# S5 set-up of a hybrid decoder trunk: rotation frames, cosine, a sum of C and the mean on other engines and in another order

## What is computed

```python
def s5_mixer(u, a_re, a_im, log_dt, b_re, b_im, c_re, c_im, d_skip, w_glu, b_glu):
    lam = lax.complex(jnp.minimum(a_re, LAMBDA_RE_MAX), a_im)      # 64 groups x 64 states
    dt = jnp.exp(log_dt)[:, None]
    lam_bar = jnp.exp(lam * dt)
    b_bar = ((lam_bar - 1.0) / lam)[:, :, None] * b_c
    bu = ...                                  # ug (16 channels of a group) x b_bar, complex
    _, states = lax.associative_scan(combine, (a, bu), axis=1)    # s_t = lam_bar * s_(t-1) + bu_t
    y = real(states) @ c_re - imag(states) @ c_im + d_skip * u
    y = gelu(y)
    z = y @ w_glu + b_glu
    val, gate = split(z, 2)
    return val * sigmoid(gate)

def reference(...):
    h = x
    h = h + s5_mixer(rmsnorm(h, g), ...) ; h = h + sq_relu_mlp(rmsnorm(h, g), ...)
    h = h + swa_sink_attention(...)      ; h = h + sq_relu_mlp(rmsnorm(h, g), ...)
    return rmsnorm(h, norm_final)
```

## Time and profile before

| | |
|---|---|
| median of 3 runs | 1054.39 us (1054.22 to 1054.98) |
| the profiled execution | 1052.76 us, of which the span of its instructions is 1050.9 us |
| busy share of the span | PE 98%, PEld 80%, POOL 66%, DVE 53%, ACT 22% |
| mean granted TensorE clock | 0.992 |
| chain that ended last, by engine | PE 86%, DVE 4%, ACT 4%, issue 2% |

### The profile page before, as it was taken

One profiled execution on the slowest core, in us unless ns is written; L12 is line 12 of the kernel. 1 busy time (PEld: TensorE's weight loads), 2 busy tenths in 40 slices (PEclk: granted clock), 3 DMA queues, 4 the chain that ended last, 5 costly groups with the idle time before them and its releaser, 6 DMA issues.

```text
span 1050.9 us, 15733 instructions
## 1 busy us (share of the span) xinstructions
PE 1026.3 (98%) x5738; PEld 839.0 (80%) x5738; DVE 560.9 (53%) x645; ACT 229.8 (22%) x512; POOL 694.8 (66%) x568
## 2 busy tenths in 40 slices
PE   9889999999999999999999999999999999999996
PEld 4677888888888888888887777888888888888886
DVE  7993446677317515613855775568761472273125
ACT  7863111110001000101312777221100010010011
POOL 8996866687667766766646330778776676677650
PEclk9899999999999999999999999999999999999998
DMA  6123332232222323222222110233223322223212
GB/s 248 39 44 124 114 102 93 77 120 100 93 89 99 100 100 100 89 94 99 100 80 100 41 51 12 80 106 101 99 96 100 100 100 100 83 97 100 100 61 80
DMA packets 35904, 97.51 MB, mean 93 GB/s; under 512 B 11144, under 2 KB 13704, under 8 KB 35600
## 3 DMA queue, kind: packets, MB, share of 16 engines
q1 hardware_dynamic: 35856, 96.83, 27.9%
HBM read 92.36 MB, written 2.10 MB: 90 GB/s over the span
## 4 chain that ended last, share of the span: by engine, by line
PE 86%; DVE 4%; ACT 4%; issue 2%; SPq 1%; DMA 1%; DVEq 0%; POOL 0%; POOLq 0%
PE ps L1265 23%; PE ps L1267 23%; PE ps L1266 23%; PE ps L1211 2%; PE ps L1213 2%; PE ps L1212 2%; SPq L314 1%; ACT s_sb L647 1%; PE ps L1422 1%; PE ps L1408 1%; PE ps L1396 1%; DMA toep<-k_even 1%; DVE negm L1028 1%; PE ps L1328 1%; PE ps L1327 1%
## 5 line engine op out<-in xcount | busy, mean ns | idle before, releaser
L438 POOL TENSOR_TENSOR w_lo<-raw,w_hi 128x1024 fp32r<-128x1024 f32 x164 | 414.8, 2529 | 13.7
L1265 PE MATMUL ps<-hid,w_hi 128*128 128x512 f32 x704 | 275.9, 392 | 0.0
L1267 PE MATMUL ps<-hid,w_lo 128*128 128x512 f32 x704 | 274.1, 389 | 0.0
L1266 PE MATMUL ps<-hid,w_hi 128*128 128x512 f32 x704 | 274.0, 389 | 0.0
L350 POOL TENSOR_TENSOR gate_sb<-gate_sb 128x1 f32<-128x1 f32 x164 | 41.0, 250 | 308.2 <-PE ps L1267 269.4
L1265 PE MATMUL ps<-act,w_hi 128*128 128x512 f32 x464 | 180.6, 389 | 0.0
L1267 PE MATMUL ps<-act,w_lo 128*128 128x512 f32 x464 | 180.5, 389 | 0.0
L1266 PE MATMUL ps<-act,w_hi 128*128 128x512 f32 x464 | 180.5, 389 | 0.0
L435 POOL TENSOR_SCALAR w_hi<-raw 128x1024 fp32r<-128x1024 f32 x164 | 173.3, 1057 | 0.0
L1267 PEld LDWEIGHTS ps<-hid,w_lo 128*128 128x128 f32 x704 | 132.1, 188 | 27.8
L1265 PEld LDWEIGHTS ps<-hid,w_hi 128*128 128x128 f32 x704 | 132.2, 188 | 27.6 <-issue 0.5
(11 more groups left out here) (218 smaller groups left out, 1062.4 us busy)
## 6 DMA issues: line engine op xcount, KB each, us to landing
raw<-panels_in SPq DMA_DIRECT2D x164, 512.0 KB, 3.2
xy<-xu_in SPq DMA_DIRECT2D x4, 512.0 KB, 7.5
out<-h SPq DMA_DIRECT2D x8, 256.0 KB, 2.2
prm<-prm_in SPq DMA_DIRECT2D x1, 1280.0 KB, 5.8
h<-x_rows_in SPq DMA_DIRECT2D x1, 1280.0 KB, 12.9
h<-x_rows_in SPq DMA_DIRECT2D x1, 768.0 KB, 7.2
dd<-dd_in SPq DMA_DIRECT2D x1, 256.0 KB, 5.8
toep<-k_even SPq DMA_DIRECT2D x4, 64.0 KB, 2.4
```

The lines of the kernel that those rows point to most:

```text
L438: nc.gpsimd.tensor_tensor(w_lo[:, s, :], raw[:, s % 2, :], w_hi[:, s, :].bitcast(F32), ALU.subtract).then_inc(w_split, 1)
L1265: mm(ps[:, bank, :], w_hi[:, s, w], x[:, 0, k, :], start=(k == 0), stop=False)
L1266: mm(ps[:, bank, :], w_hi[:, s, w], x[:, 1, k, :], start=False, stop=False)
L1267: last = mm(ps[:, bank, :], w_lo[:, s, w], x[:, 0, k, :], start=False, stop=(k == KT - 1))
```

## The change

It touches the set-up and the first two octets alone. Every other stage, every DMA and its issue stay.

- Cosine: instead of sin(pi x), its square and 1 - 2 sin^2, ACT takes Abs and then Sin with scale -2 pi and a bias of a quarter turn from a tile (`quarter`). That is one ACT operation less in each frame, one DVE operation less in the set-up (L725), and a small Sin and Square for the one power that still needs sin^2.
- The copy of the turns (`turn8`) goes ahead of the set-up's first Sin.
- Whole turns: for frames 1 to 3 DVE only rounds, and PE adds minus the whole turns in PSUM with a second matmul (`part_turns`, with the tile `minus`); ACT reads PSUM. Frame 0 is rounded and subtracted by DVE in the set-up, ahead of the input factors, and ACT does it between the squares.
- `c_sum` is formed by two matmuls on PE and a copy on ACT, not by POOL.
- The mean is reduced from PSUM bank 0 into PSUM, after `project_mul(1)`.
- `decay` is made in two halves, after the squares and in octet 1.
- The matmuls on idle data are four at the start and no others.
- New order: POOL makes the weights of octet 0 ahead of `project_im(0)`, and `minus`, the product of `dd`, `project_im(1)` and one product of octet 1 stand ahead of the wait for the mean; DVE and PE take octet 2's projection and fold ahead of `run_states(1)` and `outputs(0)`.

```diff
--- before.py
+++ after.py
...
-SETUP_ARG, SETUP_EXP, SETUP_PH, SETUP_INV, SETUP_L, SETUP_X, SETUP_MS = 3, 2, 6, 9, 15, 28, 32
-SETUP_LAG0, SETUP_R8, SETUP_TURN, SETUP_RSTD = 3, 6, 10, 11
+SETUP_ARG, SETUP_EXP, SETUP_PH, SETUP_INV, SETUP_L, SETUP_X, SETUP_MS = 3, 2, 6, 9, 14, 27, 31
+SETUP_LAG0, SETUP_R8, SETUP_TURN, SETUP_SIN, SETUP_COS, SETUP_SQ, SETUP_RSTD = 1, 6, 7, 8, 10, 12, 13
 T_DMA = 16 * J
-WARM = (5, 1, 2)
+WARM = (4, 1)
...
+QUARTER = 1.5707963
...
         sq_sum = ps[:, 4, :]
+        mean_ps = ps[:, 4, 0:2 * NK].rearrange("p (a k) -> p a k", a=2)
         stat = ps[:, 7, :]
-        phases = (t1[:], t2[:, 0], t2[:, 1], acc[:])
+        first_turns = rstd
+        whole = (t1[:], t2[:, 0], t2[:, 1], acc[:])
...
             tt(PR("b_re"), PR("b_re"), PR("g"), mul).then_inc(setup_p, 1)
             pool.wait_ge(setup_p, 2)
             tt(b_sum, PR("b_re"), PR("b_im"), add).then_inc(setup_p, 1)
-            tt(c_sum[:], PR("c_re"), PR("c_im"), add).then_inc(setup_p, 1)
+            wait(pool, s_cst, 16)
+            nc.gpsimd.tensor_scalar(minus[:], ident, -1.0, 0.0, mul, add).then_inc(negated, 1)
             wait(pool, setup_v, SETUP_L)
-            pool.wait_ge(setup_p, 4)
+            weights_mul(0, (1, 2))
+            pool.wait_ge(c_copied, 1)
             weights_mul(0, (0,))
+            weights_sum(0)
             wait(pool, setup_v, SETUP_X)
             project_im(0)
+            wait(pool, s_dd, 16)
+            tt(dd[:, 0], dd[:, 0], dd[:, 1], mul).then_inc(setup_p, 1)
             project_im(1)
-            weights_mul(0, (1, 2))
-            weights_sum(0)
+            weights_mul(1, (0,))
             wait(pool, setup_a, SETUP_RSTD)
             inputs(0)
-            wait(pool, s_dd, 16)
-            tt(dd[:, 0], dd[:, 0], dd[:, 1], mul).then_inc(setup_p, 1)
-            weights_mul(1)
+            weights_mul(1, (1, 2))
             weights_sum(1)
             inputs(1)
-            wait(pool, s_cst, 16)
-            nc.gpsimd.tensor_scalar(minus[:], ident, -1.0, 0.0, mul, add).then_inc(negated, 1)
             project_im(2)
             weights_mul(2)
...
             wait(a, setup_v, SETUP_PH)
-            act_fn(cos_l[:], ph_ps, ACT.Sin, scale=PI_).then_inc(setup_a, 1)
+            act_fn(turn8[:], ph_ps[:, :, J:J + 1].rearrange("p g a -> p (g a)"), ACT.Copy).then_inc(setup_a, 1)
             act_fn(sin_l[:], ph_ps, ACT.Sin, scale=TWO_PI).then_inc(setup_a, 1)
-            a.wait_ge(setup_a, 7)
-            act_fn(sq_ps, cos_l[:], ACT.Square).then_inc(setup_a, 1)
-            act_fn(turn8[:], ph_ps[:, :, J:J + 1].rearrange("p g a -> p (g a)"), ACT.Copy).then_inc(setup_a, 1)
+
+            act_fn(cos_l[:], ph_ps, ACT.Abs).then_inc(setup_a, 1)
+            a.wait_ge(setup_a, SETUP_COS - 1)
+            wait(a, bank_free, 4)
+            act_fn(cos_l[:], cos_l[:], ACT.Sin, scale=-TWO_PI, bias=quarter[:]).then_inc(setup_a, 1)
+            act_fn(sq_ps[:, :, 0:1].rearrange("p g a -> p (g a)"), ph_ps[:, :, 1:2].rearrange("p g a -> p (g a)"), ACT.Sin,
+                   scale=PI_).then_inc(setup_a, 1)
+            a.wait_ge(setup_a, SETUP_SQ - 1)
+            act_fn(sq_ps[:, :, 1:2].rearrange("p g a -> p (g a)"), sq_ps[:, :, 0:1].rearrange("p g a -> p (g a)"), ACT.Square
+                   ).then_inc(setup_a, 1)
...
-            a.wait_ge(setup_a, SETUP_R8)
-            act_fn(decay[:, :, 1:], r8[:].unsqueeze(2).to_broadcast([P, GP, NK - 1]), ACT.Copy).then_inc(decayed, 1)
+            def decays(n):
+                pairs = slice(n * GP // 2, (n + 1) * GP // 2)
+                act_fn(decay[:, pairs, 1:], r8[:, pairs].unsqueeze(2).to_broadcast([P, GP // 2, NK - 1]), ACT.Copy
+                       ).then_inc(decayed, 1)
+
+            def frame(c, parts=range(3)):
+
+                wait(a, frame_left, c + 1)
+                pairs = slice(8 * c, 8 * c + 8)
+                phase = (ps[:, frame_bank(c), :] if c else first_turns).rearrange("p (g k) -> p g k", k=NK)
+                if 0 in parts:
+                    act_fn(sink_[:, pairs], phase, ACT.Sin, scale=TWO_PI).then_inc(frame_a, 1)
+                if 1 in parts:
+                    act_fn(cosk[:, pairs], phase, ACT.Abs).then_inc(frame_a, 1)
+                if 2 not in parts:
+                    return
+                a.wait_ge(frame_a, 3 * c + 2)
+                act_fn(cosk[:, pairs], cosk[:, pairs], ACT.Sin, scale=-TWO_PI, bias=quarter[:]).then_inc(frame_a, 1)
+
             wait(a, turn_mm, 1)
             act_fn(turn_t[:], ps[0:8, 3, :], ACT.Copy).then_inc(turn_copied, 1)
+            wait(a, c_mm, 1)
+            act_fn(c_sum[:], ps[:, 6, :], ACT.Copy).then_inc(c_copied, 1)
             wait(a, s_prm, 16)
+            a.wait_ge(setup_a, SETUP_R8)
...
-                if o % 2 == 1 and o // 2 < SETUP_LAG0:
-                    lag0_weights(o // 2)
-
-            def frame(c):
-
-                wait(a, frame_v, 2 * c + 2)
-                pairs = slice(8 * c, 8 * c + 8)
-                phase = phases[c].rearrange("p (g k) -> p g k", k=NK)
-                act_fn(sink_[:, pairs], phase, ACT.Sin, scale=TWO_PI).then_inc(frame_a, 1)
-                act_fn(cosk[:, pairs], phase, ACT.Sin, scale=PI_).then_inc(frame_a, 1)
-                a.wait_ge(frame_a, 4 * c + 2)
-                act_fn(cosk[:, pairs], cosk[:, pairs], ACT.Square).then_inc(frame_a, 1)
-                a.wait_ge(frame_a, 4 * c + 3)
-                act_fn(cosk[:, pairs], cosk[:, pairs], ACT.Copy, scale=-2.0, bias=1.0).then_inc(frame_a, 1)
-
+                if 3 <= o <= 5:
+                    frame(0, (o - 3,))
+                if o == 6:
+                    lag0_weights(0)
+            decays(0)
...
             act_fn(rstd_u[:, 0], rstd_u[:, 1], ACT.Sqrt).then_inc(setup_a, 1)
             evacuate_v(0)
-            frame(0)
             evacuate_k(0)
             copy_p(1)
             evacuate_v(1)
+            lag0_weights(1)
             frame(1)
             for o in range(NO):
-                if 0 < o < NO - 1:
+                if 1 < o < NO - 1:
                     copy_p(o + 1)
                 if o > 0:
                     gelu(o - 1)
-                if 0 < o < NO - 1:
+                if 1 < o < NO - 1:
                     evacuate_v(o + 1)
                 if o > 1:
                     y_to_lo(o - 2)
                 if o + 1 < NO:
                     evacuate_k(o + 1)
+                if o == 1:
+                    decays(1)
                 if o > 0:
                     y_to_hi(o - 1)
                 if o == 0:
                     frame(2)
+                    copy_p(2)
+                    evacuate_v(2)
+                    lag0_weights(2)
                     frame(3)
                 elif o + 2 < NO:
                     lag0_weights(o + 2)
...
+            nc.vector.memset(quarter[:], QUARTER)
...
-            wait(v, setup_a, 9)
+            wait(v, setup_a, SETUP_SIN)
             link(tt(lim_ps, sin_l[:], mag_ps, mul))
-            link(ts(cos_l[:], sq_ps, -2.0, 1.0, mul, add))
+            wait(v, setup_a, SETUP_COS)
...
+            wait(v, setup_a, SETUP_SQ)
...
+            v.wait_ge(frame_mm, 1)
+            ts(whole[0], ps[:, frame_bank(0), :], ROUND, ROUND, add, sub).then_inc(frame_v, 1)
+            v.wait_ge(frame_v, 1)
+            tt(first_turns[:], ps[:, frame_bank(0), :], whole[0], sub).then_inc(frame_left, 1)
...
             def mean_square():
                 wait(v, sq_used, NO)
-                link(nc.vector.tensor_reduce(rstd_u[:, 0], ps[:, 6, :].rearrange("p (g k) -> p k g", k=NK), AX.X, add))
-                link(ts(rstd_u[:, 0], rstd_u[:, 0], 1.0 / D, EPS, mul, add))
-                link(nc.vector.reciprocal(rstd_u[:, 1], rstd_u[:, 0]))
+                v.wait_ge(p_done, 2)
+                link(nc.vector.tensor_reduce(mean_ps[:, 0], ps[:, 0, :].rearrange("p (g k) -> p k g", k=NK), AX.X, add))
+                link(ts(mean_ps[:, 1], mean_ps[:, 0], 1.0 / D, EPS, mul, add))
+                link(nc.vector.reciprocal(rstd_u[:, 1], mean_ps[:, 1]))
                 assert count[0] == SETUP_MS
 
             def frame(c):
 
-                turned = ps[:, frame_bank(c), :]
                 v.wait_ge(frame_mm, c + 1)
-                wait(v, frame_v, 2 * c)
-                ts(rstd[:], turned, ROUND, ROUND, add, sub).then_inc(frame_v, 1)
-                v.wait_ge(frame_v, 2 * c + 1)
-                tt(phases[c], turned, rstd[:], sub).then_inc(frame_v, 1)
+                ts(whole[c], ps[:, frame_bank(c), :], ROUND, ROUND, add, sub).then_inc(frame_v, 1)
...
-                wait(v, frame_a, 4 * (o // 2) + 4)
+                wait(v, frame_a, 3 * (o // 2) + 3)
...
+            v.wait_ge(c_copied, 1)
+            project_mul(1)
             mean_square()
-            frame(0)
-            project_mul(1)
             project_sum(1)
             frame(1)
+            frame(2)
             run_states(0)
-            frame(2)
+            project_mul(2)
+            project_sum(2)
             frame(3)
```

(54 more changed lines are left out.)

8 lines of the change are left out of this document (5 added, 3 removed).

## The result

The changed kernel took a median of 1056.12 us (1053.40 to 1057.83, 22 runs), the kernel before 1054.22 us (1052.70 to 1056.23, 22 runs): a ratio of 1.0015, with a 95% interval of 1.0008 to 1.0022. The forecast was 1054.0 with a range up to 1056.0. The change is slightly slower, by some 1.9 us (under 0.2%), where I had it slightly faster; the time lies 0.12 us above the range. The profiled execution took 1054.90 with a span of 1053.0 (before: 1052.76 and 1050.9), so span against span it is 2.1 us longer.

The account below looks back on a forecast made before the run. PE bounds the kernel, so only the GLU's start can move; POOL's -1.97 + 1.57 = -0.4 us sets it, ahead of PE's queue at 83.6. Profiled 1052.76 becomes 1052.4, median 1054.39 becomes 1054.0, range 1052.4 to 1056.0.

Parts of the forecast that it names:

- POOL's sum: POOL's queue up to the GLU: 1.97 us less work, inputs(0) 1.57 later, so -0.4; second split at 84.4.
- The costs at nothing: Set-up and first octets: c_sum on PE and ACT, frame 0, fold(0)'s wait, decay halves and cosine were priced at nothing.
- the rival at 1055.1: Set-up on ACT: a table switch costs the skill page's 2.66 us, end 1.1 us later; chance 0.03.
- PE's queue would come to the GLU at 83.6: PE's S5 queue at the full clock: ready at 84.76 - 1.2 = 83.6, ahead of POOL's 84.5.
- the 1.2 us that `lags(2)` was to gain: PE's queue, octet 2: lags(2) starts near 40.5, 1.2 us ahead of 41.70, and the chain repeats from there.
- the first stretch: PE's queue: low clock again as at 28 to 38 us puts lags(2) at 42.9 and the GLU at 85.9.
- PE's queue becomes the bound: PE between 33 and 38 us: low clock meets fold(2) and part_turns(3); GLU start +1.0, 1055.4; chance 0.26.
- The clock falls earlier: PE near 24.5 us, idle matmuls gone: lags(2) 2 to 3.5 us late, 1056.4 to 1057.9; chance 0.08.
- the step from the profiled execution to the median: Whole kernel: the median lies 1.6 us above the profiled execution, as in the kernel before, giving 1054.0.
- the forecast of the profiled execution: Whole kernel: profiled execution goes from 1052.76 to 1052.4 us, span from 1050.9 to 1050.5.

Follow-up runs that it names:

- e16: e14 with the mean's three operations on DVE ahead of project_mul(1); 1051.80 us, ratio 0.9980 to the kernel before.
- e12: e7 with its two idle matmuls ahead of the fifth attention scores instead of the first; 1050.50 us, ratio 0.9958 to the kernel before.
- e14: Changed kernel with idle matmuls in PE's long waits: fold(0), fold(2), the toep waits, the GLU, the fifth scores; 1052.53 us, ratio 0.9982 to the kernel before.
- e8: The changed kernel as it is, run and profiled once more; 1054.81 us, ratio 1.0010 to the kernel before, profiled execution 1052.38 us.
- e5: Changed kernel with two idle matmuls ahead of the first attention scores, where PE had no wait; 1056.37 us, ratio 1.0021 to the kernel before.
- e1: Changed kernel with three idle matmuls on PE behind turns(3), ahead of fold(2); 1054.04 us, ratio 1.0000 to the kernel before.
- e2: Changed kernel with one, two and one idle matmuls ahead of outputs(2), (4) and (6), into the toep waits; 1052.75 us, ratio 0.9990 to the kernel before.
- e9: Kernel before with two idle matmuls in PE's wait ahead of the fifth attention scores; 1052.94 us, ratio 0.9986 to the kernel before.
- e6: Changed kernel with one idle matmul behind turns(1), in PE's wait before fold(0); 1054.46 us, ratio 0.9998 to the kernel before.
- e15: e10 with one idle matmul more, in PE's wait ahead of fold(0); 1052.88 us, ratio 0.9988 to the kernel before.
- e4: Kernel before without its two idle matmuls ahead of sums(0); 1057.30 us, ratio 1.0020 to the kernel before.
- e7: Changed kernel, mean ahead of project_mul(1), two octet 1 products ahead of inputs(0), idle matmuls in PE's S5 and GLU waits and ahead of the first scores; 1053.65 us.
- e3: Changed kernel with the mean's three operations on DVE ahead of project_mul(1); 1053.06 us, ratio 0.9990 to the kernel before.
- e10: Changed kernel with two idle matmuls in PE's wait ahead of the fifth attention scores; 1053.67 us, ratio 0.9993 to the kernel before.
- e13: Kernel before with idle matmuls for PE's waits: lags(1), outputs(0), sums(2), the toep waits, the GLU, the fifth scores; 1053.21 us, ratio 0.9990.

## Why the prediction was right and wrong

- **POOL's sum held.** Forecast: `inputs(0)` near 22.65 behind 1.7 us of idleness, the end 0.4 earlier, at 84.4. Measured: 22.80, 1.91, 84.52 (before 84.81). Most of what `c_sum` and the gap gave did come back as the wait for the mean; e16 took 0.9 us of that wait out and gained 0.7 us in the median (1.05 in the GLU's start), e12 took out all of it and is 2.0 us below e14, on another chip.
- **The costs at nothing held.** The last sum of squares ended at 19.1 (a row of 7.97 us from 11.17) and DVE was not ready before 20.88. Abs took 0.59 (assumed 0.63), the Sin with a bias 0.71 (assumed 0.7), and no table load was added for Abs. The load between `turn8` and the Sin was no longer hidden and the Sin started at 7.00 (7.05). The Trainium skill ("ScalarE: Activation LUTs", What ACT_TABLE_LOAD costs) has 2.66 us for a switch; the rows at 5.70 and 7.00 give 1.30, as in the kernel before (21.75, and 23.05 for the next operation), so the rival at 1055.1, a load as long as that, is out.
- **The step that failed** is the part on PE's queue, "PE's queue would come to the GLU at 83.6". It took a clock at its full level from 38 us to the GLU, since the one trace had it so, and gave no price to a fall behind the waits for `toep` in that stretch. In the profiled execution the clock fell at 67 us behind 2.12 us of such a wait; PE's last S5 matmul started at 85.41 and ended at 85.9, not 83.6 (in the kernel before it started at 84.26), and the GLU at 85.76, 1.1 us later than in e8's profile, where the clock did not fall there.
- **In the same step**, the 1.2 us that `lags(2)` was to gain were carried one for one to the GLU. The profiles don't show that. From e8 to e5 `lags(2)` is 1.7 us later (41.61, 43.32) and the last S5 matmul 1.0 (83.48, 84.47); from e8 to e1 it is 0.4 earlier (41.24) and that matmul 2.1 (81.40), with shorter waits for `toep` between. The prediction had PE's queue ready at 83.6 at the full clock and at 85.9 with the first stretch; it was ready at 81.9 (e1) and 84.0 (e8). No run isolates why those waits shrink.
- **The rival "PE's queue becomes the bound"** (0.26, 1055.4) came true in its result, the GLU starting behind L1241 and not behind a split, with +0.85 where I had +1.0; its mechanism was half right. The low clock did meet `fold(2)` and `part_turns(3)` as it said, but this cost nothing at the GLU (84.64 in e8, 84.70 in e2). The fall that cost was another, which no rival named. "The clock falls earlier" (0.08) is seen in one profile (e5, at 22 us, with `fold(0)` and not from 24.5); together with the stretch at 35 us it costs 0.2 us, not 2.0 to 3.5.
- **The term that set the number** is the step from the profiled execution to the median, which I took over from the kernel before, 1.6 us. It is no constant: e9 shows it to be mostly the attention's low stretch (1.39 us in the rows at 586), present in some executions of either kernel. In the changed kernel the stretch at 67 comes on top: 1052.4 + 1.1 + 1.4 = 1054.9, the profiled 1054.90. e14 and e8's profile, 1052.4, show that the forecast of the profiled execution was right where the clock holds. But these terms explain 1054.9, which lies inside the range, and not the median of 1056.12; the second median, 1054.81, lies inside it too. The forecast's nearness to the second, 0.8 us, is luck: the sum had no term for the stretch at 67, and the step of 1.6 us stood in for the others.
- **Still open.** What makes the group at 1056.5 to 1057.8 (12 of the changed kernel's 34 executions) is not profiled; the trace of after has three stretches and 1054.90. Other low stretches that cost time are seen in single profiles, in `outputs(6)` (e6) and in the GLU (1.5 us in e1, 2.6 in e15). The share of the idle matmuls that the change took away is clear in the kernel before (2.9 us), and in the changed one not shown (0.7 us in the mean, twice, within the intervals). Nor is it shown that the changed kernel has more low stretches than the kernel before; e9's profile has two in the S5 as well.

## What to carry to other kernels

Before a median is forecast from one trace, list the waits of TensorE (most falls that cost time here came behind 1.9 us of waiting and more, but the next section has falls without such a wait), and ask of each what a low clock right behind it would cost; a wait that is slack for late inputs is also a place where the clock may fall, so spread in the times is a term of the sum and not noise. Filling such waits with idle matmuls of no more than the wait's length narrowed the times from 4.4 us to 0.7 here and made 1 us steps visible; the same matmuls where PE had no wait cost their full length. And the queue that is ahead should be made no earlier than the one that bounds it: what was won on PE alone (the profiles of e1 and e15) was lost again in a wait ahead of the dense work.

## What the runs showed of the hardware that I had not expected

- The granted clock falls behind a wait of PE in one execution and stays in another of the same program: 2.12 us ahead of `outputs(4)` and a fall at 67 in the changed kernel, 2.09 us and none when it was run again, 2.33 us and none in the kernel before; 1.95 us for `qT` and a fall in the profiles of after, e1, e4, e6 and e7, none in those of before, e2, e3, e5 and e8. Of the waits for `toep`, those up to 1.9 us were followed by no fall in these profiles; of the longer ones those of 1.98 (e6), 2.12, 2.49 (e4) and 2.68 us (e10) were, and those of 1.96 (e5), 2.09 (e8), 2.33, 2.34 (e3) and 2.38 us (e9) were not.
- A long wait is not needed. In the kernel before the clock is low from 28 us on, where PE begins to wait only 0.78 us, and in e13 it falls at 28 with that wait filled by an idle matmul; in e9 it falls at 30.3, 1.6 us behind a wait of 0.98. What stands ahead in all three are short groups of matmuls, those of 8 rows among them.
- What PE does in such a stretch takes twice its time: 1.98 instead of 1.09 us for 16 matmuls of `outputs`. In dense work one of 3 to 4 us cost 1.4 us (the rows from 586 on) to 1.5 us (those at 67, and the GLU in e1), one of 6.7 us in the GLU 2.6 (e15).
- It also falls in the middle of dense work that follows a wait: in e1 from 86 us, 1.2 us behind the start of the GLU's matmuls.
